# Projecting 32 sample tokens of two mixers in plain fp32 by four column groups

## The chip, the cores and the metric

The kernel runs on one core of a Trainium2 chip. The metric is the device time of one execution in microseconds (us), lower is better. Engines are named PE (TensorE), DVE (VectorE), ACT (ScalarE), POOL (GpSimd) and SP (SyncE, which here only issues DMAs).

## The reference

One inference step of a two-layer encoder for two request groups: 512 prompt tokens and 32 sample tokens with a cache of 256 past rows. What matters here is the start of each mixer:

```python
h = _rmsnorm(x, norm_mix[l]) * (1.0 + sc1) + sh1
# even layer: 4 differential-attention heads, 8 stick-breaking heads
proj = h @ w_in_even        # (T, 1024) @ (1024, 3072)
# odd layer: 16 forgetting-attention heads, and 16 gate logits
q, k, v, fl = jnp.split(h @ w_in_odd, [FOX_W, 2 * FOX_W, 3 * FOX_W], axis=-1)
logf = jax.nn.log_sigmoid(fl + b_f)
```

The same weights project both groups. Attention, output projection, a mixture of 16 experts and a final norm follow; their code does not change, apart from one count on which the output weights' load waits. Everything is fp32 in and out.

## The kernel before

**Product.** The 544 tokens are five row tiles: four of 128 prompt tokens (t = 0 to 3) and one with the 32 sample tokens (t = 4, `NT`), padded to 128 columns. The 3072 weight columns are cut into `NB` = 8 blocks of `BW` = 384 (128 each of q, k, v). A product of one tile with one block is numbered n = 5b + t. It is made to fp32 accuracy from three products of rounded parts (`split_product`, L563 to L565): high by high, high by low, low by high, over 8 slices k of the contraction, so 24 matmuls with 128 stationary and 384 moving columns, into `bank[n % 2]`. The sample tile takes the same 24 as a prompt tile. ACT rounds each raw weight quarter (`fuse_high`, L612), DVE makes the rest (`fuse_low`, L618); the raw block lies in one buffer, `fu_raw`, that SP fills with 8 DMAs (`fuse_load`, L603) once the lows of the block before are made. ACT copies the tiles t = 0, 2, 4 of a block out of the banks (L661), DVE the tiles 1 and 3 (L668).

**Order.** Everything is ordered by hand. Each mixer has a lead and then 40 units u = 5i + t (block i, tile t). In the lead (`lead_pe`) the normed rows are turned by PE transposes, in the order sample tile, then prompt tiles 0 to 3, each turned tile rounded into `hT` (ACT, `row_high`, L494) and `hT2` (DVE, `row_low`, L500); products 0 to 4 are put between. In the odd layer the gate logits (`gate_logits`) stand before product 4. Then in unit u PE does the attention of unit u while product u + 6 is cut into three pieces (slices 0-2, 2-6, 6-8; 0-4, 4-6, 6-8 where t = 0) which stand between attention steps: next scores, piece, turn or later sums, piece, values, piece. So the product of the sample tile of block i + 2 stands in the unit t = 3 of block i. Attention uses L849, L863, L886 (differential), L895 to L949 (stick-breaking) and L1447 to L1485 (forgetting); ACT's copies L1041, L1076 and L1550 feed the values.

**Beside it.** The conditioning rows of coming layers are computed in the same units by `ada_matvec` (L326) and `ada_sum` (L332): 8 plain fp32 matmuls of 32 stationary and 512 moving columns in four column groups, whose weights (2 MB a chunk) also come through SP's queue. Each plain fp32 matmul stands as two records in the trace. In the even mixer POOL's queue carries cache loads and stores of new rows; in the odd one SP's.

Of the kernel before, what the change touches and what calls it, by code (L numbers as in the profile page):

```python
# [21 lines left out]
P = 128  # L22
# [53 lines left out]
def encoder_step(nc, a, out, rope_dram):  # L76
    ctx = ExitStack()
    with ctx:
# [51 lines left out]
        upto = sb("upto", [P, P])  # L130
# [8 lines left out]
        c_in = sb("c_in", [P, 2, KD])  # L139
        ss = sb("ss", [P, 8])  # L140
# [58 lines left out]
        def setup_pool(pool):  # L199
# [7 lines left out]
            pool.memset(upto[:, :], 1.0)  # L207
# [11 lines left out]
            for m in (ident, ident_b):  # L219
# [5 lines left out]
                               pattern=[[1, P]], channel_multiplier=-1)  # L225
            pool.affine_select(out=upto[:, :], in_=upto[:, :], compare_op=ALU.is_ge, fill=0.0, base=0,
# [204 lines left out]
        NORM = sems("norm", "square", "rstd", "scaled", "shifted", "tr", "ev_a", "ev_v", "self", "gain", "shift_v", "pad")  # L431
# [70 lines left out]

        def row_pool(pool, l):
            s, o = NORM, 2 * l
            for flat in (hT_flat, hT2_flat):
                pool.tensor_copy(r32(flat[:, KD * TOK:HT_LEN]), ones[:, 0:P - DEC]).then_inc(s["pad"], 1)
# [26 lines left out]
        def lead_pe(pe, l, last_logits=None):  # L533

            row_turn(pe, l, 0)
            row_turn(pe, l, 1)
            row_turn(pe, l, 2)
            for t in range(TILES):
                row_evicted(pe, l, min(t + 1, TILES - 1))
                if t == NT:  # L540
                    pe.wait_ge(NORM["pad"], 2 * l + 2)
                    if last_logits:
                        last_logits()
                fuse_product(pe, l, t, 0, KD)
                if t + 3 < TILES:
                    row_turn(pe, l, t + 3)

# [29 lines left out]
        FU = sems("fu", "raw0", "raw1", "hi", "lo", "mm", "ev_a", "ev_v")  # L577
# [4 lines left out]
        fu_lo = [ring_flat[:, 2 * KD * BW * i + KD * BW:2 * KD * BW * (i + 1)] for i in range(2)]  # L582
        by_row = lambda v: v.rearrange("p (k c) -> p k c", k=KD)
# [21 lines left out]
        def fuse_high(act, l, b, q):  # L605
# [3 lines left out]
            if b >= 2:  # L609
                act.wait_ge(FU["mm"], TILES * (g_b - 1))  # L610
# [9 lines left out]
        def fuse_product(pe, l, n, k0, k1):  # L620

            if n >= NB * TILES:
                return
            b, t = n // TILES, n % TILES
            hi, lo = r32(by_row(fu_hi[b % 2])), r32(by_row(fu_lo[b % 2]))
            for k in range(k0, k1):
                if t == 0 and k % 2 == 0:
                    pe.wait_ge(FU["lo"], 4 * (NB * l + b) + k // 2 + 1)
                if k == 0 and n >= 2:
                    fuse_rows_out(pe, l, n - 2)  # L630
# [4 lines left out]

        def fuse_rows_out(eng, l, n):

            g_b, t = NB * l + n // TILES, n % TILES
            if t % 2 == 0:
                eng.wait_ge(FU["ev_a"], 3 * g_b + t // 2 + 1)  # L640
            else:
                eng.wait_ge(FU["ev_v"], 2 * g_b + t // 2 + 1)

# [12 lines left out]
        def fuse_rows_act(act, l, n):  # L656
            b, t = n // TILES, n % TILES
            if n < NB * TILES and t % 2 == 0:
                act.wait_ge(FU["mm"], UNITS * l + n + 1)
                fuse_rows_free(act, l, b)  # L660
                act.activation(fu_rows[b % 2][0:rows(t), t, :], bank[n % 2][0:rows(t), 0:BW], ACT.Copy).then_inc(FU["ev_a"], 1)  # L661

        def fuse_rows_dve(dve, l, n):
            b, t = n // TILES, n % TILES
            if n < NB * TILES and t % 2 == 1:
                dve.wait_ge(FU["mm"], UNITS * l + n + 1)
                fuse_rows_free(dve, l, b)
                dve.tensor_copy(fu_rows[b % 2][0:rows(t), t, :], bank[n % 2][0:rows(t), 0:BW]).then_inc(FU["ev_v"], 1)  # L668
# [75 lines left out]
        def even_pool(pool):  # L744
# [13 lines left out]
            def store(b):  # L758
                pool.wait_ge(FU["ev_a"], 3 * b + 3)
                pool.wait_ge(FU["ev_v"], 2 * b + 2)  # L760
# [37 lines left out]
        def even_pe(pe):  # L798
# [7 lines left out]
            def turn_q_k(i):  # L806
# [4 lines left out]
                else:  # L811
                    pe.wait_ge(FU["ev_a"], 3 * i + 2)
                    pe.wait_ge(FU["ev_v"], 2 * i + 2)
# [4 lines left out]
            def turn_rest(i):  # L818
                if i < N_DIFF:
                    pe.wait_ge(F0["roped"], 2 * i + 2)  # L820
                else:
                    pe.wait_ge(FU["ev_a"], 3 * i + 3)
# [199 lines left out]
        def even_act(act):  # L1022
# [109 lines left out]
            row_high(act, 0, 2)  # L1132
            fuse_rows_act(act, 0, 0)
# [5 lines left out]
            fuse_rows_act(act, 0, 4)  # L1139
            q_out(0)  # L1140
            late_out(0)
            for u in range(UNITS):
                i, t = u // TILES, u % TILES
# [1480 lines left out]
```

## Time and profile before

| | |
|---|---|
| median of 3 runs | 1740.81 us (1735.86 to 1748.72) |
| profiled execution, its own time | 1750.45 us |
| its span in the trace | 1748.7 us |
| PE busy | 1486.2 us (85%) |
| DVE busy | 1032.4 us (59%) |
| ACT busy | 865.5 us (49%) |
| POOL busy | 489.7 us (28%) |
| TensorE granted clock, mean | 0.924 |

Times inside the execution are counted from the span's start. The even mixer runs from about 50 to 418 us, the odd one from about 898 to 1279 us. "Busy" PE records overlap, because matmuls are pipelined: a matmul's length in the trace holds its latency, and what it costs is the distance from its start to the start of the next.

### The profile page before, as it was taken

The numbers are of one execution on the slowest core, as the hardware profiler recorded it, in microseconds if no ns is written. First come the engines' busy times: TensorE is split into PE (matmuls) and PEld (weight loads), VectorE is DVE, ScalarE is ACT, GpSimd is POOL, SyncE is SP. The second block draws the span as 40 slices with busy tenths as digits, with TensorE's granted clock in tenths as the row PEclk, the third lists the DMA queues.
The fourth block names the chain that finished last, engine by engine and source line by source line (L and its number), as shares of the span: only waits on it lengthen the run. The fifth ranks groups of instructions, "written<-read, shape, count | busy, mean of one in ns | idle before, by whom it ended". The sixth has DMA issues, their size and how long they took to land.

```text
span 1748.7 us, 22798 instructions
## 1 busy us (share of the span) xinstructions
PE 1486.2 (85%) x7979; PEld 1162.0 (66%) x7979; DVE 1032.4 (59%) x1345; ACT 865.5 (49%) x1512; POOL 489.7 (28%) x379
## 2 busy tenths in 40 slices
PE   3499999997947999999937899999889399999981
PEld 0387777764735777877727677777567277878770
DVE  0555442224446988988956443333363568888995
ACT  2233334445124777777733333333341267788772
POOL 1200111110104666656521000000001155656650
PEclk8699999998967999999968999999989599999995
DMA  8435553133044899989970333443420479999984
GB/s 279 147 120 180 187 170 104 68 124 106 1 195 154 337 351 356 369 342 354 357 249 12 98 104 104 129 136 114 155 75 36 167 263 344 367 367 364 335 314 170
DMA packets 148608, 358.62 MB, mean 205 GB/s; under 512 B 18660, under 2 KB 80868, under 8 KB 122420
## 3 DMA queue, kind: packets, MB, share of 16 engines
q1 hardware_dynamic: 136184, 333.25, 52.7%
q0 software_dynamic: 12352, 24.40, 3.8%
q8 instruction: 45, 0.74, 0.2%
q14 instruction: 27, 0.22, 0.0%
HBM read 341.87 MB, written 33.56 MB: 215 GB/s over the span
## 4 chain that ended last, share of the span: by engine, by line
PE 65%; DVE 12%; issue 7%; ACT 6%; DMA 5%; SPq 2%; DVEq 1%; POOL 0%; POOLq 0%; ACTq 0%; PEldq 0%; PEld 0%
PE bank L563 17%; PE bank L565 15%; PE bank L564 15%; DVE ring_r L1945 4%; DMA ring<-in_w_gate 2%; PE bank L326 2%; ACT work_r L1938 2%; PE bank L1447 2%; PE bank L1485 1%; PE bank L676 1%; PE bank L332 1%; PE bank L1462 1%; PE bank L2231 1%; PE bank L919 1%; PE bank L558 1%
## 5 line engine op out<-in xcount | busy, mean ns | idle before, releaser
L564 PE MATMUL bank<-ring_r,arena_r 128*128 128x512 f32 x816 | 323.6, 397 | 0.0
L563 PE MATMUL bank<-ring_r,hT_r 128*128 128x384 f32 x640 | 239.9, 375 | 1.6 <-ACT hT_r L494 1.6
L564 PE MATMUL bank<-ring_r,hT_r 128*128 128x384 f32 x640 | 217.0, 339 | 0.0
L565 PE MATMUL bank<-ring_r,work_r 128*128 128x384 f32 x640 | 217.0, 339 | 0.0
L1945 DVE TENSOR_TENSOR ring_r<-ring,work_r 128x1024 fp32r<-128x1024 f32 x102 | 177.2, 1763 | 28.2 <-ACT work_r L1938 28.2
L1945 DVE TENSOR_TENSOR ring_r<-ring,arena_r 128x1024 fp32r<-128x1024 f32 x96 | 166.4, 1771 | 29.3 <-ACT arena_r L1938 29.3
L564 PEld LDWEIGHTS bank<-ring_r,arena_r 128*128 128x128 f32 x816 | 157.3, 193 | 31.1
L1945 DVE TENSOR_TENSOR ring_r<-ring,hT_r 128x1024 fp32r<-128x1024 f32 x108 | 155.1, 1464 | 25.1 <-ACT hT_r L1938 24.3
L1938 ACT ACTIVATE hT_r<-ring 128x1024 fp32r<-128x1024 f32 x144 | 144.3, 1054 | 47.3 <-DMA ring<-in_w_gate 41.5
L563 PEld LDWEIGHTS bank<-ring_r,hT_r 128*128 128x128 f32 x640 | 121.7, 190 | 43.0 <-issue 39.1
L1938 ACT ACTIVATE work_r<-ring 128x1024 fp32r<-128x1024 f32 x136 | 136.6, 1059 | 6.9 <-DMA ring<-in_w_up 6.8
L1938 ACT ACTIVATE arena_r<-ring 128x1024 fp32r<-128x1024 f32 x128 | 126.8, 1052 | 21.6 <-DMA ring<-in_w_down 21.3
L1889 POOL TENSOR_TENSOR arena<-arena,bc 128x1024 f32<-128x1024 f32 (+1 forms) x6 | 14.3, 2382 | 434.9 <-DVE arena L1875 434.9
L563 PE MATMUL bank<-hT_r,arena_r 128*128 128x512 f32 x288 | 123.2, 428 | 8.9 <-DVE arena_r L2386 5.6
L564 PEld LDWEIGHTS bank<-ring_r,hT_r 128*128 128x128 f32 x640 | 122.2, 191 | 1.2 <-issue 0.7
L565 PEld LDWEIGHTS bank<-ring_r,work_r 128*128 128x128 f32 x640 | 121.3, 190 | 0.0
L565 PE MATMUL bank<-hT_r,arena_r 128*128 128x512 f32 x288 | 118.4, 411 | 0.0
L2421 POOL TENSOR_TENSOR ring_r<-ring,arena_r 128x1024 fp32r<-128x1024 f32 x32 | 86.3, 2696 | 90.9 <-ACT arena_r L1938 90.9
L563 PE MATMUL bank<-work_r,arena_r 128*128 128x512 f32 x272 | 109.2, 402 | 0.0
L2421 POOL TENSOR_TENSOR ring_r<-ring,hT_r 128x1024 fp32r<-128x1024 f32 x36 | 92.4, 2566 | 54.0 <-ACT hT_r L1938 40.4
L563 PE MATMUL bank<-arena_r 128*128 128x512 f32 x256 | 100.9, 394 | 6.7 <-DVE ring_r L1945 6.6
L565 PE MATMUL bank<-work_r,arena_r 128*128 128x512 f32 x272 | 106.4, 391 | 0.0
(356 smaller groups left out, 2880.3 us busy)
## 6 DMA issues: line engine op xcount, KB each, us to landing
ring<-in_w_gate SPq DMA_DIRECT2D x68, 1024.0 KB, 6.8
ring<-in_w_up SPq DMA_DIRECT2D x68, 1024.0 KB, 7.4
ring<-in_w_down SPq DMA_DIRECT2D x68, 1024.0 KB, 7.5
bc<-in_w_ada SPq DMA_DIRECT2D x40, 1024.0 KB, 6.8
bc<-in_w_in_even SPq DMA_DIRECT2D x64, 192.0 KB, 4.0
bc<-in_w_in_odd SPq DMA_DIRECT2D x64, 192.0 KB, 3.6
ring<-in_w_ada SPq DMA_DIRECT2D x4, 2048.0 KB, 12.3
arena<-moe_out SPq DMA_DIRECT2D x8, 1024.0 KB
```

Source lines behind the costliest of these rows:

```text
L326: last = nc.tensor.matmul(acc[32 * q:32 * q + 32, :], silu_c[:, 4 * h + q, :], ada_w[h][:, q, :], start=h == 0, stop=h == 1)
L332: nc.tensor.matmul(acc[0:32, :], pick[:, :], ada_part(pre), start=True, stop=True).then_inc(AD["sum"], 1)
L558: last = nc.tensor.matmul(acc, wr[:, k, :], hT[:, k, cols(t)], start=k == 0, stop=k == KD - 1)
L563: nc.tensor.matmul(acc, rows_hi, w_hi, start=first, stop=False)
L564: nc.tensor.matmul(acc, rows_hi, w_lo, start=False, stop=False)
L565: return nc.tensor.matmul(acc, rows_lo, w_hi, start=False, stop=last)
L676: last = nc.tensor.transpose(out_bank[0:np_, c:c + r], src, ident[0:r, 0:r])
L919: last = nc.tensor.matmul(b[:, 0:n], neg_from[:, :], s[:, 0:n], start=False, stop=True, skip_group_check=True)
L1447: nc.tensor.matmul(fx_bank(u, h)[0:r, 0:n], fx_qT[i % 2][half, cols(t)], fx_kT[i % 2][half, k0:k0 + n], start=True, stop=False)
L1938: act.activation(r32(piece(m_high[v], q)), piece(m_low[v], q), ACT.Copy).then_inc(MO[f"hi_{c}"], 1)
L1945: dve.tensor_tensor(r32(piece(m_low[v], q)), piece(m_low[v], q), f32(piece(m_high[v], q)), ALU.subtract).then_inc(MO[f"lo_{c}"], 1)
L2421: pool.tensor_tensor(r32(piece(m_low[v], 1)), piece(m_low[v], 1), f32(piece(m_high[v], 1)), ALU.subtract).then_inc(MO[f"lop_{c}"], 1)
```

## The change

The sample tile is no longer projected with the 24 split matmuls. DVE copies the turned sample rows unrounded into `sample_T` (two copies in each lead). A new `fuse_sample` multiplies them with the raw fp32 block: for each slice k four matmuls, each with the 32 sample tokens stationary and a quarter (96) of the block's columns moving, written to partitions 32q to 32q + 31 of one bank. The raw block therefore has to be there until that product is done: `fuse_load` waits for it too. The sample product moves one block ahead: that of block 0 is made in the lead after the third turn, in bank 6, and that of block b + 1 stands where the sample tile of block b stood (n = 5b + 4, cut into the same three pieces); the last such place, in the unit t = 3 of block 6, is empty. ACT evicts it with four copies of 32 by 96, `sample_rows`, at the start of the unit t = 0 one block later. The gate logits move before product 3. In the odd lead DVE evicts tile 3 after the last two weight quarters, and copies the first k rows (`k_out(0)`) after the gate chain. Counts of semaphores follow. Unused `upto` is dropped.

```diff
 def row_sample(dve, l):
+    for half in range(2):
+        dve.wait_ge(s["ev_a"], EV_A[o] + half + 1)
+        dve.tensor_copy(sample_T[:, 4 * half:4 * half + 4, :], row_turned(0, half)).then_inc(s["smp"], 1)
@@ lead_pe
             row_turn(pe, l, 1)
+            pe.wait_ge(NORM["smp"], 2 * l + 2)
             row_turn(pe, l, 2)
-            for t in range(TILES):
-                row_evicted(pe, l, min(t + 1, TILES - 1))
-                if t == NT:
-                    pe.wait_ge(NORM["pad"], 2 * l + 2)
-                    if last_logits:
-                        last_logits()
+            fuse_sample(pe, l, 0, bank[6], 0, KD)
+            for t in range(NT):
+                row_evicted(pe, l, t + 1)
+                if t == NT - 1 and last_logits:
+                    last_logits()
                 fuse_product(pe, l, t, 0, KD)
                 if t + 3 < TILES:
                     row_turn(pe, l, t + 3)
+            fuse_product(pe, l, NT, 0, KD)
@@ fuse_load
                 sp.wait_ge(FU["lo"], 4 * g_b)
+                sp.wait_ge(FU["smp"], g_b)
@@ fuse_product
+            if b + t // NT >= NB:
                 return
+            if k0 == 0 and n >= 2:
+                fuse_rows_out(pe, l, n - 2)
+            if t == NT:
+                fuse_sample(pe, l, b + 1, bank[n % 2], k0, k1)
+                return
+        def fuse_sample(pe, l, b, acc, k0, k1):
+            w = by_row(fu_raw)
+            for k in range(k0, k1):
+                if k % 4 == 0:
+                    pe.wait_ge(FU[f"raw{k // 4}"], 64 * (NB * l + b) + 64)
+                for q in range(4):
+                    last = nc.tensor.matmul(acc[DEC * q:DEC * (q + 1), 0:SW], sample_T[:, k, :], w[:, k, SW * q:SW * (q + 1)],
+                                            start=k == 0, stop=k == KD - 1)
+            if k1 == KD:
+                last.then_inc(FU["smp"], 1)
+        def sample_rows(act, l, b, acc):
+            act.wait_ge(FU["smp"], NB * l + b + 1)
+            fuse_rows_free(act, l, b)
+            for q in range(4):
+                act.activation(fu_rows[b % 2][0:DEC, NT, SW * q:SW * (q + 1)], acc[DEC * q:DEC * (q + 1), 0:SW],
+                               ACT.Copy).then_inc(FU["ev_s"], 1)
@@ even_act and fox_act, the units
+                if t == 0 and 1 <= i < NB - 1:
+                    sample_rows(act, l, i + 1, sample_bank(i + 1))
                 fuse_rows_act(act, l, u + TILES)
@@ fox_dve
             fuse_low(dve, 1, 1, 1)
-            fuse_rows_dve(dve, 1, 3)
...
             fuse_low(dve, 1, 1, 3)
-            k_out(0)
+            fuse_rows_dve(dve, 1, 3)
...
             dve.drain().then_inc(FG["dve"], 1)
+            k_out(0)
             maxima(0)
```

## Rows read from the trace of the kernel before

**Rows 1.** Windows over the units of both mixers: window, length, busy time by engine, clock, DMA.

```profile
103.00:263.00 160.00, 160.00 (x984) 122.39 (x985) 77.96 (x204) 59.55 (x169) 18.25 (x28) 1.00 0.50 170
...
975.00:1263.00 288.00, 280.52 (x1910) 212.15 (x1910) 106.80 (x256) 104.40 (x315) 0.00 (x0) 0.98 0.38 121
```

**Rows 2.** Timeline of PE, odd mixer, unit t = 3 of block 2: start, length, instruction.

```profile
1084.15 0.45 PE L563 MATMUL bank<-ring_r,hT_r 128*128 128x384 f32 x1
...
1085.32 1.04 PE L1462 MATMUL bank<-ident,arena 128*128 128x128 f32 x8
...
1087.26 0.45 PE L563 MATMUL bank<-ring_r,hT_r 128*128 128x384 f32 x1
...
1089.56 1.09 PE L1485 MATMUL bank<-arena 128*64 128x128 f32 x16
1090.58 0.44 PE L563 MATMUL bank<-ring_r,hT_r 128*128 128x384 f32 x1
...
1092.80 0.27 PE L676 MATMUL bank<-ident,arena 128*128 128x128 f32 x1
```

**Rows 3.** Timeline of ACT, odd mixer, same unit.

```profile
1086.01 1.09 ACT L1550 ACTIVATE arena<-bank 128x512 f32<-128x512 f32 x2 [0.18 <-PE bank L1462]
```

**Rows 4.** Timeline of PE, differential part of the even mixer, unit t = 3 of block 1.

```profile
169.46 0.42 PE L563 MATMUL bank<-ring_r,hT_r 128*128 128x384 f32 x1
...
171.64 1.05 PE L886 MATMUL bank<-arena 128*128 128x128 f32 x8
172.45 0.42 PE L563 MATMUL bank<-ring_r,hT_r 128*128 128x384 f32 x1
...
173.68 0.62 PE L332 MATMUL bank<-bc,pick 128*32 128x512 f32 x1
```

**Rows 5.** Timeline of ACT, same unit.

```profile
169.74 0.60 ACT L1041 ACTIVATE arena<-bank 128x512 f32<-128x512 f32 x1
```

**Rows 6.** Timelines of PE and ACT, stick-breaking part, unit t = 3 of block 5.

```profile
333.22 0.63 PE L563 MATMUL bank<-ring_r,hT_r 128*128 128x384 f32 x1
...
335.70 1.08 PE L942 MATMUL bank<-arena 128*64 128x512 f32 x4
...
333.71 0.60 ACT L1076 ACTIVATE arena<-bank 128x512 f32<-128x512 f32 x1 [0.85 <-PE bank L929]
```

**Rows 7.** Timeline of PE: one conditioning product in four column groups, and what follows.

```profile
125.92 1.92 PE L326 MATMUL bank<-bc,silu_c 128*32 128x512 f32 x16
127.78 0.44 PE L563 MATMUL bank<-ring_r,hT_r 128*128 128x384 f32 x1
```

**Rows 8.** Timeline of PE: the short values of a sample unit in two column groups.

```profile
1097.13 0.66 PE L1485 MATMUL bank<-arena 128*64 128x32 f32 x12
1097.71 0.49 PE L1447 MATMUL bank<-arena 64*128 64x128 f32 x4
```

**Rows 9.** Sources: all weight loads of L326, count, durations in ns (min/median/max).

```profile
L326 PEld LDWEIGHTS bank<-bc,silu_c x320: 106/110/178, 110.2 to 1262.3; 128*32 128x32 f32 x160
```

**Rows 10.** Timeline of PE, lead of the even mixer: third turn and first product.

```profile
71.66 1.97 PE L526 MATMUL bank<-ident,arena 128*128 128x128 f32 x8 [1.65 <-POOL arena L511]
75.24 0.66 PE L563 MATMUL bank<-ring_r,hT_r 128*128 128x384 f32 x1 [1.62 <-ACT hT_r L494]
```

**Rows 11.** Timelines of PE, lead of the odd mixer: product 0, next turn, first scores.

```profile
932.62 0.67 PE L563 MATMUL bank<-ring_r,hT_r 128*128 128x384 f32 x1
...
937.95 1.03 PE L526 MATMUL bank<-ident,arena 128*128 128x128 f32 x8
...
975.29 0.38 PE L1447 MATMUL bank<-arena 64*128 64x128 f32 x2 [4.21 <-ACT logf L1599]
```

**Rows 12.** Window over product 0 of that lead.

```profile
932.60:938.00 5.40, 5.40 (x27) 5.37 (x26) 5.33 (x6) 2.40 (x6) 0.00 (x0) 0.78 0.00 0
```

**Rows 13.** Timelines of SP's queue and ACT: a raw block's 8 loads, and their first use.

```profile
173.28 4.16 SPq L603 DMA_DIRECT2D bc<-in_w_in_even  x8
...
183.61 0.85 ACT L612 ACTIVATE ring_r<-bc 128x768 fp32r<-128x768 f32 x1
```

More of the change, by code:

```diff
@@ L429, in encoder_step @@
         junk = arena[:, 14336:15360]
-        NORM = sems("norm", "square", "rstd", "scaled", "shifted", "tr", "ev_a", "ev_v", "self", "gain", "shift_v", "pad")
+        NORM = sems("norm", "square", "rstd", "scaled", "shifted", "tr", "ev_a", "ev_v", "self", "gain", "shift_v", "smp")
         NORM_NO = {"norm_mix0": 0, "norm_ffn0": 1, "norm_mix1": 2, "norm_ffn1": 3}
@@ L505, in row_pool @@
             for flat in (hT_flat, hT2_flat):
-                pool.tensor_copy(r32(flat[:, KD * TOK:HT_LEN]), ones[:, 0:P - DEC]).then_inc(s["pad"], 1)
+                pool.tensor_copy(r32(flat[:, KD * TOK:HT_LEN]), ones[:, 0:P - DEC])
             for j in (0, 2, 4):
@@ L657, in fuse_rows_act, with sample_bank @@
             b, t = n // TILES, n % TILES
-            if n < NB * TILES and t % 2 == 0:
-                act.wait_ge(FU["mm"], UNITS * l + n + 1)
+            if n < NB * TILES and t in (0, 2):
+                act.wait_ge(FU["mm"], NT * (NB * l + b) + t + 1)
                 fuse_rows_free(act, l, b)
-                act.activation(fu_rows[b % 2][0:rows(t), t, :], bank[n % 2][0:rows(t), 0:BW], ACT.Copy).then_inc(FU["ev_a"], 1)
+                act.activation(fu_rows[b % 2][:, t, :], bank[n % 2][:, 0:BW], ACT.Copy).then_inc(FU["ev_a"], 1)
         def fuse_rows_dve(dve, l, n):
             b, t = n // TILES, n % TILES
-            if n < NB * TILES and t % 2 == 1:
-                dve.wait_ge(FU["mm"], UNITS * l + n + 1)
+            if n < NB * TILES and t in (1, 3):
+                dve.wait_ge(FU["mm"], NT * (NB * l + b) + t + 1)
                 fuse_rows_free(dve, l, b)
-                dve.tensor_copy(fu_rows[b % 2][0:rows(t), t, :], bank[n % 2][0:rows(t), 0:BW]).then_inc(FU["ev_v"], 1)
+                dve.tensor_copy(fu_rows[b % 2][:, t, :], bank[n % 2][:, 0:BW]).then_inc(FU["ev_v"], 1)
+        def sample_bank(b):
+            return bank[6] if b == 0 else bank[(TILES * b - 1) % 2]
         def fx_bank(u, h):
@@ L1601, in fox_act @@
                 i, t = u // TILES, u % TILES
+                if t == 0 and 1 <= i < NB - 1:
+                    sample_rows(act, 1, i + 1, sample_bank(i + 1))
                 fuse_rows_act(act, 1, u + TILES)
@@ L1664, in fox_dve @@
             row_shift(dve, 1, 1)
+            row_sample(dve, 1)
             row_low(dve, 1, 0)
```

62 lines of the change are left out of this document (34 added, 28 removed).

## The prediction

> **What bounds the kernel now.** I read the windows over the mixers first. In the differential units PE is busy for the whole window, in the units of the odd mixer for 280.5 of 288 us, both at the full clock, while DVE, ACT and the DMA engines are busy for half of it or less [rows 1]. What remains is to see whether the piece that the change shortens is really paid for by PE, so I went on to the timeline of PE in a unit t = 3, the unit whose filler is the sample product. In the odd mixer (block 2) its first piece runs from 1084.15 to the turn at 1085.32, 1.17 us; its middle piece from 1087.26 to the values at 1089.56, 2.30 us; its last one follows the values and merges with the first piece of the next product, 1090.58 to 1092.80, 2.22 us for both [rows 2]. In the even mixer the last piece stands alone: the middle one costs 2.18 us, the last 1.23 us [rows 4]. No idle time is marked before any of these. Then ACT, to see how early what PE needs next is there: the values of the odd unit need two copies that end at 1087.10, and PE comes for them 2.46 us later [rows 3, 2]. The differential ones need a copy that ends at 170.34, PE comes at 171.64 [rows 5, 4]; the stick-breaking ones one that ends at 334.31, PE comes at 335.70 [rows 6]. So PE bounds these units, with 1.3 to 2.5 us of slack behind the middle piece.
>
> **What the new product costs.** The nearest rows are the conditioning products: the same form, 32 stationary columns, four column groups, plain fp32, 8 matmuls as 16 records, but 512 moving columns. The whole takes 127.78 - 125.92 = 1.86 us [rows 7]. Were the records run one after another, each would have 0.12 us for 512 columns, less than the product's records of 384 columns take at the full clock (12 in 2.18 us, 0.18 each [rows 4]); so I read it that four run side by side, and there are four rounds. I split the 1.86 us into 0.15 for going into and out of the groups and four rounds of 0.427. With 96 columns a round is 0.427 x 96 / 512 = 0.080 us. The sample product has 64 records, 16 rounds, 1.28 us; cut into three pieces (4, 8 and 4 rounds) it pays 0.15 three times: pieces of 0.47, 0.79, 0.47, **1.73 us** in all. That is the lower bound, short of an overlap still better than in rows 7. The upper one is from the shortest grouped records of the trace, values with 32 columns in two groups: 12 records, six rounds, in 0.58 us; less the 0.15, 0.072 a round, where streaming would ask for 0.027 [rows 8]. If that is four instructions (two loads, two matmuls) being issued, a round of eight takes 0.144 us, and the product 2.75 us. I take 1.73, since rows 7 have the same groups, the same eight instructions a round, and the nearer length.
>
> The Trainium skill, TensorEngine Tiling (Array Packing), Instruction Overhead, puts some 60 cycles on every matmul; taken as an estimate, 64 records one behind the other at 25 ns would be 1.6 us plus the three entries, 2.05 us, and the forecast would be 4 us later. Rows 7 show no such charge beside the streaming, though their long matmuls could hide it.
>
> **Steady state, odd mixer.** Per sample product: before, 1.17 + 2.30 + 2.22 = 5.69 us with the next product's first piece; after, 1.73 + 1.2 for that piece alone (as the first piece here). 2.76 us saved. Does the slack hold? The turn ends and `ada_sum` (0.98 us from its start to the next piece [rows 2]) stands between it and the piece, so the values come 1.5 us earlier with respect to ACT's copies, out of 2.46: yes. Six such places: 16.6 us. The seventh place is empty now: all 5.69 go but 1.2, 4.5 us, with PE then just behind ACT. Together **21.1 us**.
>
> **Even mixer.** Differential, four places: first piece 1.15 by likeness, 0.68 saved; last 1.23 - 0.47 = 0.76. The middle piece could fall by 1.39, but slack is 1.30 less about 0.1 for the signal, so 1.2. 2.64 us each, 10.6. Stick-breaking, two places: slack 1.39, the same 1.3 for the middle, 2.7 each, 5.4. The empty place: 1.15 + 1.23 + 1.3 = 3.7. Together **19.7 us**.
>
> **Leads.** In the even one product 4 (24 records at 0.18, 4.2 us) gives way to the sample product of block 1 in one piece, 1.28 + 0.15 = 1.4: 2.8 saved. That of block 0 is new. PE sits idle 1.62 us between the third turn (from 71.66, about 2 us) and product 0 at 75.24 [rows 10], and it comes there, at the lower clock, 1.2 GHz (the eight transposes before it take 1.97 us, later ones 1.03 [rows 10, 11]): 2.56 + 0.3 = 2.9 us, 1.3 more than the gap. Product 0 itself now runs partly at that clock (5.33 us in the odd lead at a mean 0.78 [rows 11, 12] against 4.2), so 1.2 us of it comes back if the clock rises during the new product instead. Net 2.5 saved.
> In the odd lead there is no gap: the sample product of block 0 delays product 0 by 2.9, DVE's two copies before the third turn by 0.4, the clock gives back 1.2: 2.1 us later. The gate logits move ahead of product 3, 4.2 earlier, and product 4 is gone. The first scores at 975.29 waited 4.21 us for ACT's last copy of the gate chain [rows 11], so that chain decides, and it starts 2.1 earlier. In it `k_out(0)`, which stood ahead of the forget chain on DVE and waits for PE's transposes, moves behind it; the eviction of tile 3 stands there instead and comes earlier. I price this at 0 to 4 us and take 1.9: 4.0 in sum, at which PE's own work (product 3, sample, product 5, transposes) ends at the same time as the chain. Both leads **6.5 us**.
>
> **Costed at nothing.** The four evictions on ACT (about 0.6 us) stand before a copy for which ACT waits on PE anyway; the bank that they free is needed a piece later. DVE's copies in the even lead fall where it waits for POOL. SP: the raw block's load waits now for the sample product, too. Its eight issues, 173.28 to 177.44, begin when the sample product's last piece (172.45 to 173.68) is ending [rows 4, 13]; that piece will end about 2.6 us sooner, so the old gate stays the later one. First use is at 183.61 [rows 13], 6.2 us after the last issue; minus 2.6 there are 3.6 left for it. Behind the load stand on SP the conditioning weights, in the odd mixer past rows too. In both leads the load of block 1 moves behind the first sample product, with over 5 us in hand. The stores wait for sample rows that come a block earlier. Without `upto` POOL's setup is shorter, off the path.
>
> **Sum.** 21.1 + 19.7 + 6.5 = 47.3, I take 47. The profiled execution 1750.45 becomes 1703; it stands 9.6 above the median of the runs shown, and from the median, 1740.81, I get **1694 us**. Bounds: at 2.75 us a product 14 places lose 1 us and the first two about 1 each, 16 us less; leads at their worst 4 less: 1714. Better: no stall behind the middle pieces and the full chain gain, 5 more: 1689. The runs shown spread over 13 us, 6 either way: 1683 to 1718 as range, the far end short of the two bounds together with the spread.
>
> **Rivals.**
> *The groups run one after another* (slower). If matmuls in one bank on the same columns exclude each other, and each pays rows 8's 0.045 over its streaming: 64 x 0.125 + 0.45 = 8.45 us against 4.7. Twelve places +3.8, one lead product +4, the first ones +6 each, less the 8.2 of the empty places: +53, 1794 us. It turns slower from about 5.2 us a product; serial at bare streaming, 5.6, is 1750. Against: rows 7 write the same bank's same columns. 4%.
> *Loads of weights don't hide* (1719). A load of 32 columns lasts 0.110 us [rows 9]; if each round waits for it, a round is 0.190 and the product 3.5 us, 25 less gained. Against: rows 7 leave no room for four such waits within 0.15 us. 4%. The Trainium skill, TensorE: Matmul & The Clock Gate, The mechanism, says that weight loads overlap running matmuls only if the row group differs (it also allows the background buffer); all groups here share the rows, so by the strict reading this rival would hold, and the trace speaks against it.
> *The units are bound by their chain* (1717). ACT, DVE and PE pass a unit's data around; if shorter pieces meet it everywhere, only first and last pieces gain, 1.4 x 12, plus 6.5 from leads. For: slack is small in the even mixer; against: rows 2 and 3. 6%.
> *The raw load comes late* (1721). If the sample product's end gates the load and the rest of SP's queue comes behind, ACT blocks in `fuse_high` ahead of the probabilities, 2 us a block over 14 blocks. Against: the 3.6 us. 5%.
> The forecast's mechanism: 81%.
>
> **Chances.** A measurement of this kernel tells about 1%, 17 us, from no change. Faster by more: forecast and three rivals, less some of their lower ends, 92%. Within 1%: 4%. Slower: 4%.
>
> **What would show it.** Right: 64 records a product, starting in fours; 1.3 to 1.4 us in the leads; units t = 3 shorter by 2.7; the odd mixer's first scores 4 us sooner after its third turn. Wrong: L1485, L886 or L942 with idle time before them in unit t = 3; L612 waiting for DMA beyond block 0's one; rounds of over 0.1 us. The forecast fails if a round takes more than 0.144 us, or if a lead's chain eats what the units give.

## The result and the profile after

The changed kernel takes 1697.26 us (median of 4 runs, 1694.26 to 1700.78) against 1741.49 us for the kernel before on the same chip (4 runs, 1735.86 to 1748.72). The ratio is 0.9741, with a 95% interval of 0.9715 to 0.9767: 44 us less, where 47 were forecast.

The first lines of the profile's page show less PE work in more instructions (before: 1486.2 us in 7979).

```profile
span 1699.0 us, 24152 instructions
PE 1439.4 (85%) x8611; PEld 1115.0 (66%) x8619; DVE 1022.3 (60%) x1349; ACT 872.2 (51%) x1560; POOL 491.1 (29%) x377
```

The profiled spans differ by 49.7 us. To see how much of that is the change, I cut PE's timeline at eight starts, four in each mixer: the first turn, the first and the last `ada_matvec` (it recurs in the same units of every block, so it marks the block's period), and the first matmul of the output projection.

| us | before | after | difference | forecast |
|---|---|---|---|---|
| even mixer, lead (first turn to first `ada_matvec`) | 43.16 | 40.95 | -2.2 | -2.5 |
| even mixer, units (to the last `ada_matvec`) | 295.88 | 277.63 | -18.3 | -19.7 |
| odd mixer, lead | 75.81 | 73.45 | -2.4 | -4.0 |
| odd mixer, units | 266.17 | 244.22 | -22.0 | -21.1 |
| ends of both (to the output projection) | 40.25 | 41.24 | +1.0 | 0 |
| **mixers together** | 721.3 | 677.5 | **-43.8** | -47.3 |
| all other work up to PE's last matmul | 988.1 | 982.0 | -6.1 | 0 |

The last row cannot be put down to the change. Nothing there was edited in any kernel of this study, apart from the one count on which the output weights' load waits, and it came out between 972.6 and 988.7 us over all of them. A few microseconds of the change's effect could hide in that. So below, mechanisms are judged by the sum over the mixers, and the medians only where they differ by more.

The mixers scatter too, and one place where they do is the last period of the odd units, the one with the empty place. Windows over it in the kernel before and in the changed one (columns as in [rows 1]; the clock is the third number from the end):

```profile
1228.15:1260.60 32.45, 28.75 (x205) 19.66 (x204) 11.10 (x30) 11.30 (x38) 0.00 (x0) 0.93 0.34 119
...
1188.40:1216.07 27.67, 22.74 (x180) 14.70 (x179) 11.09 (x30) 10.71 (x37) 0.00 (x0) 1.00 0.56 196
```

The changed kernel ran it wholly at the full clock, and the kernel before did not. Four of the experiments below leave this stretch as it is and still did not run it wholly at the full clock: there it took 28.5 to 29.0 us at a mean of 0.91 to 0.94, and 29.50 at 0.87. So some 1 us of the 22.0 in the odd units is the clock of this execution and not the smaller product. (The last period of the even units is alike: a mean of 0.95 before, 1.00 after.)

**The unit that the change shortens.** Timeline of PE, changed kernel, odd mixer, unit t = 3 of block 2 (columns as in [rows 2], whose unit this is):

```profile
1055.85 0.54 PE L652 MATMUL bank<-bc,sample_T 128*32 128x96 f32 x16
1056.32 1.09 PE L1505 MATMUL bank<-ident,arena 128*128 128x128 f32 x8
1057.34 0.62 PE L329 MATMUL bank<-bc,pick 128*32 128x512 f32 x1
1057.36 0.37 PE L652 MATMUL bank<-bc,sample_T 128*32 128x96 f32 x6
1057.80 0.59 PE L329 MATMUL bank<-bc,pick 128*32 128x512 f32 x1
1058.22 0.82 PE L652 MATMUL bank<-bc,sample_T 128*32 128x96 f32 x26
1058.98 1.09 PE L1528 MATMUL bank<-arena 128*64 128x128 f32 x16
1060.00 0.54 PE L652 MATMUL bank<-bc,sample_T 128*32 128x96 f32 x16
1060.47 0.44 PE L567 MATMUL bank<-ring_r,hT_r 128*128 128x384 f32 x1
```

From start to start, the first piece costs 0.47 us (1055.85 to 1056.32) where it was 1.17, and the last one 0.47. No idle time is marked before the values, L1528. The period of a block falls from 38.95 to 36.09 us, six times by 2.86. In the stick-breaking part it falls from 44.42 to 41.73, in the differential one from 38.33 to 36.25 us.

In the differential unit the values now do wait, for ACT's copy of the turn. Timeline of PE from the next unit's scores (L889) on, and then ACT's exponentials of those scores (L1071) and its copy, block 1 as in [rows 4, 5]:

```profile
162.03 0.68 PE L889 MATMUL bank<-arena 64*32 64x288 f32 x4
162.64 0.54 PE L652 MATMUL bank<-bc,sample_T 128*32 128x96 f32 x16
163.11 0.66 PE L903 MATMUL bank<-ident,arena 128*128 128x128 f32 x4
163.69 0.87 PE L652 MATMUL bank<-bc,sample_T 128*32 128x96 f32 x32
164.87 1.16 PE L926 MATMUL bank<-arena 128*128 128x128 f32 x8 [0.31 <-ACT arena L1081]
165.96 0.54 PE L652 MATMUL bank<-bc,sample_T 128*32 128x96 f32 x16
166.31 1.02 PE L329 MATMUL bank<-bc,pick 128*32 128x512 f32 x2
...
163.28 0.49 ACT L1071 ACTIVATE arena<-bank,small 32x288 f32<-32x288 f32 x1 [6.31 <-DVE small L1225]
...
164.15 0.18 ACT L1071 ACTIVATION_READ_ACCUMULATOR arena<-bank,small 32x1 f32 x1
164.25 0.57 ACT L1081 ACTIVATE arena<-bank 128x512 f32<-128x512 f32 x1
```

The copy ends at 164.82, the values start at 164.87. The copy stands on ACT right behind the exponentials, and these waited for DVE's maxima of the scores (L1225). So what the values wait for begins with the scores and not with the turn: they start 2.84 us after the scores (162.03 to 164.87), where the kernel before, whose copy had 1.3 us to spare, came to them after 4.29. Its scores (the values start at 171.64 [rows 4]):

```profile
167.35 0.68 PE L849 MATMUL bank<-arena 64*32 64x288 f32 x4
```

**The whole product in one piece**, in the two leads: at the lower clock in the first place, at the full one in the second. Timelines of PE, even and odd mixer, each with the matmul that follows:

```profile
72.54 2.79 PE L652 MATMUL bank<-bc,sample_T 128*32 128x96 f32 x64
75.26 0.69 PE L567 MATMUL bank<-ring_r,hT_r 128*128 128x384 f32 x1
...
943.08 1.53 PE L652 MATMUL bank<-bc,sample_T 128*32 128x96 f32 x64
944.54 0.44 PE L567 MATMUL bank<-ring_r,hT_r 128*128 128x384 f32 x1
```

That is 2.72 and 1.46 us, against 4.2 for the 24 split matmuls. The sources view of the line has the length of its weight loads (ns, minimum/median/maximum):

```profile
L652 PEld LDWEIGHTS bank<-bc,sample_T x1024: 106/110/178, 72.5 to 1168.5; 128*32 128x32 f32 x171
```

64 loads of 110 ns are 7.0 us, in a product that lasts 1.46. So the loads run beside each other and beside the matmuls, though all four groups use the same rows.

**The start of the odd units.** Timeline of PE, lead and first units, without the product's rows:

```profile
951.40 0.49 PE L1490 MATMUL bank<-arena 64*128 64x128 f32 x4 [0.49 <-issue]
...
962.34 0.69 PE L1528 MATMUL bank<-arena 128*64 128x128 f32 x4 [5.62 <-ACT arena L1593]
```

The scores no longer wait for the gate chain (4.21 us in [rows 11]). But the values of unit 0 wait 5.62 us. The next fence, ACT and SP's queue of the same stretch, says for what:

```profile
960.20 0.84 ACT L618 ACTIVATE ring_r<-bc 128x768 fp32r<-128x768 f32 x1 [6.87 <-DMA bc<-in_w_in_odd]
961.85 0.44 ACT L1593 ACTIVATE arena<-bank 128x128 f32<-128x128 f32 x2
...
951.33 0.38 SPq L1418 DMA_DIRECT2D out_fox_logf_p<-logf  x1
953.86 0.50 SPq L1409 DMA_DIRECT2D out_fox_v_s<-arena  x1
954.46 4.09 SPq L609 DMA_DIRECT2D bc<-in_w_in_odd  x8
```

ACT rounds the first quarter of raw block 2 ahead of the turned probabilities, and block 2's load stands on SP behind the stores of the gate rows and of the first state; the gate rows are what the gate chain ends with. The kernel before has the same stall, 3.49 us long:

```profile
985.63 0.44 PE L1485 MATMUL bank<-arena 128*64 128x128 f32 x4 [3.49 <-ACT arena L1550]
...
983.49 0.84 ACT L612 ACTIVATE ring_r<-bc 128x768 fp32r<-128x768 f32 x1 [6.24 <-DMA bc<-in_w_in_odd]
```

### The profile page after: what moved, and what is told of

It reads as the page before. It is cut to its first block, busy times and chain, and to the rows that moved or that the text cites. A ratio compares the mean times of both kernels' runs of the same rounds, so it can differ in the third digit from the quotient of the medians.

```text
span 1699.0 us, 24152 instructions
## 1 busy us (share of the span) xinstructions
PE 1439.4 (85%) x8611; PEld 1115.0 (66%) x8619; DVE 1022.3 (60%) x1349; ACT 872.2 (51%) x1560; POOL 491.1 (29%) x377
## 4 chain that ended last, share of the span: by engine, by line
PE 64%; DVE 11%; issue 8%; DMA 7%; ACT 6%; SPq 2%; DVEq 1%; POOLq 0%; ACTq 0%; PEldq 0%; POOL 0%; PEld 0%
PE bank L567 15%; PE bank L569 14%; PE bank L568 14%; DVE ring_r L1992 3%; DMA ring<-in_w_gate 3%; PE bank L323 2%; PE bank L1490 2%; PE bank L1528 2%; ACT work_r L1985 2%; PE bank L652 1%; PE bank L717 1%; DMA ring<-in_w_up 1%; PE bank L1505 1%; PE bank L329 1%; PE bank L2278 1%
## 5 line engine op out<-in xcount | busy, mean ns | idle before, releaser
L567 PE MATMUL bank<-ring_r,hT_r 128*128 128x384 f32 x512 | 191.9, 375 | 0.0
L569 PE MATMUL bank<-ring_r,work_r 128*128 128x384 f32 x512 | 173.1, 338 | 0.0
L568 PE MATMUL bank<-ring_r,hT_r 128*128 128x384 f32 x512 | 172.9, 338 | 0.0
L1992 DVE TENSOR_TENSOR ring_r<-ring,hT_r 128x1024 fp32r<-128x1024 f32 x108 | 150.1, 1418 | 26.8 <-ACT hT_r L1985 25.9
L567 PEld LDWEIGHTS bank<-ring_r,hT_r 128*128 128x128 f32 x512 | 96.9, 189 | 30.9 <-issue 28.5
L567 PE MATMUL bank<-arena_r 128*128 128x512 f32 x256 | 100.9, 394 | 6.1 <-DVE ring_r L1992 5.8
L569 PE MATMUL bank<-arena_r 128*128 128x512 f32 x256 | 99.8, 390 | 0.0
L568 PEld LDWEIGHTS bank<-ring_r,hT_r 128*128 128x128 f32 x512 | 97.4, 190 | 0.8 <-issue 0.7
```

The costliest lines, as they stand in the source:

```text
L567: nc.tensor.matmul(acc, rows_hi, w_hi, start=first, stop=False)
L568: nc.tensor.matmul(acc, rows_hi, w_lo, start=False, stop=False)
L569: return nc.tensor.matmul(acc, rows_lo, w_hi, start=False, stop=last)
L1992: dve.tensor_tensor(r32(piece(m_low[v], q)), piece(m_low[v], q), f32(piece(m_high[v], q)), ALU.subtract).then_inc(MO[f"lo_{c}"], 1)
```

## The experiments

The runs behind the first comparison came in three groups, each on one chip beside the kernel before. One column group, gate logits back, load early and first sample product earlier ran beside 1745.43 us; whole product in the middle piece, before with load early, load early with gate logits back and all three beside 1744.02; the three marked "again" beside 1743.50. The last two columns are of the one profiled execution.

| kernel | median us | ratio to before | mixers | all other |
|---|---|---|---|---|
| before (profile) | | | 721.3 | 988.1 |
| changed | 1697.26 | 0.9741 [0.9715, 0.9767] | 677.5 | 982.0 |
| changed again | 1696.53 | 0.9723 [0.9696, 0.9750] | 676.9 | 980.3 |
| one column group | 1757.02 | 1.0060 [1.0029, 1.0091] | 739.8 | 981.8 |
| gate logits back | 1696.37 | 0.9704 [0.9647, 0.9762] | 677.2 | 972.6 |
| load early | 1684.82 | 0.9632 [0.9594, 0.9671] | 670.2 | 979.4 |
| load early again | 1691.40 | 0.9696 [0.9668, 0.9724] | 668.9 | 978.5 |
| load early, gate logits back | 1694.50 | 0.9716 [0.9676, 0.9757] | 674.5 | 988.4 |
| first sample product earlier | 1691.16 | 0.9677 [0.9636, 0.9717] | 672.8 | 976.1 |
| whole product in the middle piece | 1691.62 | 0.9697 [0.9662, 0.9733] | 672.6 | 979.6 |
| before, with load early | 1744.15 | 0.9988 [0.9949, 1.0028] | 717.1 | 985.2 |
| load early, first earlier, middle | 1685.01 | 0.9656 [0.9622, 0.9690] | 661.9 | 988.7 |
| the same three again | 1683.17 | 0.9655 [0.9630, 0.9681] | 666.8 | 977.2 |

**One column group.** The same 32 matmuls with the same operands, all four quarters written to partitions 0 to 31 (at other columns of the bank), where ACT's copies then read them.

```diff
-                    last = nc.tensor.matmul(acc[DEC * q:DEC * (q + 1), 0:SW], ...,
-                                            start=k == 0, stop=k == KD - 1)
+                    last = nc.tensor.matmul(acc[0:DEC, SW * q:SW * (q + 1)], ...,
+                                            start=k == 0 and q == 0, stop=k == KD - 1 and q == 3, ...)
```

> All four quarters of a sample product are written to the same partitions 0 to 31, at different columns of the bank, so that all 64 records use one column group and can only run one after another; all else as in the changed kernel. Theory (four groups run side by side, PE is what the units pay for): a record streams 0.080 us, a product takes at least 5.1 us instead of 1.46 in one piece, 14 products in the units and leads on PE's path cost 3.7 more each, the two first ones up to 5: about +55 to +65 us on the changed kernel, 1750 to 1765, so slightly slower than before. Rival (the groups contribute little, the gain comes from the smaller padding alone): 1697 to 1710. Rival (the units are bound by their chain, not by PE): under +25.

Measured: 1757.02 us, and periods of 40.01 (odd), 39.80 (differential) and 45.66 us (stick-breaking), all longer than before the change (38.95, 38.33, 44.42). Timeline of PE, odd unit t = 3, of block 1, middle piece and values:

```profile
1058.08 2.80 PE L652 MATMUL bank<-bc,sample_T 128*32 128x96 f32 x32
1060.82 1.09 PE L1528 MATMUL bank<-arena 128*64 128x128 f32 x16
```

32 records take 2.73 us, 0.085 each, and 64 in the lead 5.40 us against 1.46: the four groups do run side by side, 3.7 times faster than one. Here too 64 loads of 110 ns, 7.0 us, fit into 5.40. It is the rival "groups one after another", realised: it needed about 5.2 us a product to turn slower, this one takes 5.4 to 5.6 and is slower. Without the groups the smaller product gains nothing.

**Gate logits back.** Behind product 3 again, with DVE's eviction of tile 3 ahead of the gate chain.

```diff
-                if t == NT - 1 and last_logits:
-                    last_logits()
                 fuse_product(pe, l, t, 0, KD)
...
+            if last_logits:
+                last_logits()
             fuse_product(pe, l, NT, 0, KD)
```

> The changed kernel with the gate logits back behind product 3 (ahead of the sample product of block 1), DVE's eviction of tile 3 back ahead of its wait for them. Theory (the gate chain decides when the odd mixer's units start, PE's own lead work ends just with it): the gate chain starts 4.2 us later, product 3 no longer covers it, the first scores come 3 to 4 us later: about 1700.5, PE idle 3 to 4 us before the first scores. Rival (what bounds the start of the odd mixer is the load of block 2's raw weights, which stands on SP behind the gate rows): the same 3 to 4 us, since that load waits for the same rows. Rival (the move was worth nothing): within 1 us of the changed kernel.

Measured: no difference (mixers 677.2 against 677.5). The first scores do come 2.7 us later after the first turn (55.70 us instead of 53.01), but the first `ada_matvec` does not (73.35 against 73.45). Timeline of PE, and windows from the first scores to the turn of unit 0 and from the values to the first `ada_matvec`:

```profile
944.39 0.80 PE L1490 MATMUL bank<-arena 64*128 64x128 f32 x4 [3.25 <-ACT logf L1643]
...
954.79 0.44 PE L1528 MATMUL bank<-arena 128*64 128x128 f32 x4 [2.23 <-ACT arena L1593]
```

```profile
944.39:951.13 6.74, 6.74 (x28) 5.52 (x29) 1.89 (x7) 1.08 (x5) 0.00 (x0) 0.52 0.69 184
954.79:962.04 7.25, 7.25 (x49) 5.70 (x49) 3.83 (x9) 2.47 (x7) 0.00 (x0) 1.00 0.76 273
```

The same two windows of the changed kernel:

```profile
951.40:955.29 3.89, 3.89 (x29) 3.27 (x30) 1.80 (x7) 1.08 (x5) 0.00 (x0) 1.00 0.57 152
962.34:971.84 9.50, 9.50 (x48) 6.87 (x48) 3.82 (x9) 2.46 (x7) 0.00 (x0) 0.73 0.49 184
```

The wait for the chain is back (3.25 us), and the wait behind it is 3.39 us shorter. But that alone is not why nothing changes. The load stands behind the gate rows, which come later too, and so the values come 2.15 us later after the first turn (66.10 for 63.95), much as the rival on the load had it. What gives this back is the clock. Here it was low behind the first wait (6.74 us for 3.89), a stretch behind which PE waits for the load anyway, and full behind the values. In the changed kernel it was low behind the long wait of the values, which costs 2.25 us (9.50 for 7.25). The expectation missed, since it did not price the clock.

**Load early.** Raw block 2 issued ahead of SP's wait for the gate rows (the place in the loop goes).

```diff
+            fuse_load(sp, 1, 2)
             sp.wait_ge(FG["act"], FG_ACT["rows"])
...
-                if i + 2 < NB:
+                if 1 <= i < NB - 2:
                     fuse_load(sp, 1, i + 2)
```

> The changed kernel with the raw load of block 2 of the odd mixer issued before SP waits for the gate rows, not after the stores of block 0. Theory A (that load is what keeps the units from starting: PE stands for 6.9 us minus one piece in unit 0 because ACT waits for it ahead of its probabilities): the stall goes, 6 to 8 us less, about 1690; the next thing late may be the conditioning weights of that block. Theory B (the lead gave less than forecast because of the new first sample product at the lower clock): this changes nothing, within 1.5 us of the changed kernel.

Measured: the stall is gone, and the first `ada_matvec` comes 65.06 us after the first turn, 8.4 sooner. That is more than the stall of 5.62 us: behind it, values to `ada_matvec` take 7.23 us at a mean clock of 1.00, where the changed kernel took 9.50 at 0.73. The load is issued 6.6 us ahead of the gate rows; SP's queue, then PE's values of unit 0, with no idle time marked:

```profile
938.51 4.09 SPq L609 DMA_DIRECT2D bc<-in_w_in_odd  x8
945.12 0.38 SPq L1419 DMA_DIRECT2D out_fox_logf_p<-logf  x1
...
950.44 0.33 PE L1529 MATMUL bank<-arena 128*64 128x128 f32 x2
```

The mixers gain 7.3 us, since the last period of the odd units gives 1.8 back, at the lower clock shown above. The median fell by 12.4; the repeat below gave 5.1, so the rest of the 12.4 is not the load's.

**Load early in the kernel before.** The same edit there.

> The kernel before, with one edit: in the odd mixer the raw load of block 2 is issued ahead of the wait for the gate rows, not behind the gate rows' and the first state's store. Theory: the wait of the first unit of block 0 for that load was there before the change (TensorE waited 3.5 us in it), so the edit alone brings the kernel before from 1741 to about 1736, and takes the first ada_matvec of the odd mixer 4 to 6 us nearer to its first turn (75.81 us before). Rival: the stall is one of the changed kernel alone, made by its earlier start of the scores: 1741 and 75.8.

Measured: the lead falls from 75.81 to 70.45 us and the mixers by 4.1 us. The median doesn't show it (0.9949 to 1.0028 holds both 0 and 4 us). So the stall is older than the change, as the theory has it; that the whole kernel gets faster by it stays unconfirmed.

**Load early, gate logits back.** Both edits, to see what the move of the gate logits is worth once the load doesn't hide it.

> The changed kernel with the raw load of block 2 early (1684.82 in the run before) and, in addition, the gate logits back behind product 3 and DVE's eviction of tile 3 back ahead of the gate chain. Theory: the move of the gate logits is worth what the first scores come later without it (2.7 us), and the load alone had hidden that: with the load early it shows, so 1687 to 1688, first turn to first ada_matvec 67.5 to 68 instead of 65.06. Rival: the move is worth nothing in either, since another wait (TensorE waits for the evicted block 0 or its copies) stands in that place: 1685, 65.

Measured: 71.06 us from first turn to first `ada_matvec` instead of 65.06, 6.0 later, twice the theory's 2.7. Timeline of PE, and then the window from the first scores to the turn of unit 0 (columns as in [rows 1]), in this kernel:

```profile
957.77 0.80 PE L1491 MATMUL bank<-arena 64*128 64x128 f32 x4 [3.25 <-ACT logf L1644]
```

```profile
957.77:964.52 6.75, 6.75 (x28) 5.53 (x29) 3.45 (x11) 2.84 (x10) 0.00 (x0) 0.52 0.68 193
```

The same window of the kernel with the load early alone:

```profile
945.19:949.07 3.88, 3.88 (x28) 3.27 (x29) 2.36 (x8) 2.67 (x10) 0.00 (x0) 1.00 0.61 163
```

The same 28 records take 6.75 us instead of 3.88, at a mean granted clock of 0.52, nearly all at the lower level, instead of 1.00. The wait of 3.25 us for the gate chain costs itself (the scores come 3.1 later) and 2.9 more behind it.

**First sample product earlier.** In both leads it stands ahead of the third turn, where PE waits anyway.

```diff
             pe.wait_ge(NORM["smp"], 2 * l + 2)
-            row_turn(pe, l, 2)
             fuse_sample(pe, l, 0, bank[6], 0, KD)
+            row_turn(pe, l, 2)
```

> The changed kernel with the sample product of block 0 put ahead of the third turn, where PE has nothing to do, in both leads. Theory B (the first sample product delays product 0 at the lower clock): in the odd lead all 2.7 us of it come back, in the even one some 1 to 2: 3 to 5 us less, about 1693. Theory A (the odd lead's end is set by the gate chain and the load behind it): the gate chain starts earlier by the same 2.7, so the same 3 to 5 us. Rival (the clock falls back between the turns and product 0 so that it pays what the move saves): within 1.5 us.

Measured: mixers 4.7 us less, the odd lead 3.1 and the even one 1.6 of it; product 0 of the odd mixer comes 14.39 us after the first turn instead of 17.41, nearly back at the 14.00 of before. There the sample product no longer delays anything; what PE waits for is POOL:

```profile
901.28 1.97 PE L529 MATMUL bank<-ident,arena 128*128 128x128 f32 x8 [3.38 <-POOL arena L514]
```

**Whole product in the middle piece.** In the units t = 3 of both mixers all eight slices stand in the middle place, none in the first and last (the odd mixer's lines are shown).

```diff
-                    k = 4 if t == 0 else 2
+                    whole = n % TILES == NT
+                    k = 0 if whole else 4 if t == 0 else 2
                     fuse_product(pe, 1, n, 0, k)
...
-                    fuse_product(pe, 1, n, k, 6)
+                    fuse_product(pe, 1, n, k, KD if whole else 6)
```

> In the unit t = 3 of every block in both mixers, the whole sample product stands in the unit's middle piece (all eight k, where the changed kernel has k 0-1, 2-5 and 6-7 in three places). Theory: each place where the sample records stand among other TensorE work costs its neighbours 0.1 to 0.3 us (in the changed kernel the stall inside the middle piece of 1.175 us, the turns before it 0.587 and the values behind it 1.088 us, against 0.80, 0.36 and 0.81 without it). One place instead of three then gives 0.7 to 0.9 us per differential unit, 0.3 per stick-breaking and per odd unit: the periods of the differential blocks go from 36.25 to about 35.5 us, and the total from 1697 to about 1692. Rival: the places cost nothing and the missing 0.56 us per differential block are waits of the chain, which stay: 1697, periods as in the changed kernel. Rival: the unit's chain had the pieces as its cover, and waits open where they stood: 1700.

Measured: 5.0 us less in the mixers, but a good part of it is not the edit's. The periods fall by 0.33 (differential, where 0.75 was expected), 0.27 (odd) and 0.24 us (stick-breaking), some 3 us over all places. Yet the units as a whole are only 1.6 us shorter, as the last odd period took 28.79 us at a mean clock of 0.94. The other 3.4 us lie in the leads and ends, which the edit does not touch, and are taken for scatter. Timeline of PE and then ACT's copy, differential unit of block 1:

```profile
161.48 0.68 PE L889 MATMUL bank<-arena 64*32 64x288 f32 x4
162.09 0.66 PE L903 MATMUL bank<-ident,arena 128*128 128x128 f32 x4
162.67 1.53 PE L652 MATMUL bank<-bc,sample_T 128*32 128x96 f32 x64
164.32 1.16 PE L926 MATMUL bank<-arena 128*128 128x128 f32 x8
...
163.69 0.57 ACT L1083 ACTIVATE arena<-bank 128x512 f32<-128x512 f32 x1
```

No idle time is marked before the values, but they still start 0.06 us after the copy ends (164.26), and 2.84 us after the scores, as in the changed kernel. So scores, DVE, ACT and copy still decide when the values start. What the edit gives here is the last piece, 0.35 us in the changed kernel (165.96 to 166.31), which now stands in time that PE had to wait through. In the odd units, which did not wait, 0.27 us is about what two entries less are worth at the prediction's 0.15 each.

The turn still takes 0.58 us (162.09 to 162.67) and the values 1.09. In the kernel before, the values took 0.81 us, and the turn 0.35, from this row to the piece at 169.46 [rows 4]:

```profile
169.11 0.60 PE L863 MATMUL bank<-ident,arena 128*128 128x128 f32 x4
```

So full-width matmuls next to the sample records take 0.2 to 0.3 us more than next to the split ones, wherever the product is cut.

**All three.** Early load, first sample product earlier, whole product in the middle.

> The changed kernel with the raw load of block 2 early, the leads' sample product ahead of the third turn of rows, and the sample product of the unit t = 3 whole in the middle piece. If the three add up: 12.4 less for the load, 3 to 6 less for the leads, 5 less for the middle piece, so about 1675 to 1681. Rival: the lead's product 0 ahead only moves TensorE into a wait for the gate chain, and the last odd interval gives back 1 to 2 us: 1682 to 1685.

The median, 1685.01 us, was no better than that of the early load alone on another chip, while the mixers were at 661.9, 15.6 below the changed kernel (the three edits' own gains, 7.3, 4.7 and 5.0, add up to 17.0). Only runs on one chip could settle that, hence the last three.

> The changed kernel itself, once more. In the runs so far the two mixers (from the first turn of a lead to the start of the output projection) took 721.3 us before and 677.5 us after the change, and agreed to 0.3 us between profiles where nothing in them was edited, while everything outside the mixers took 972.6 to 988.7 us in profiles whose edits don't touch it. Theory: that is a property of single executions, so here the mixers take 677 to 678 again, the rest anything from 972 to 989, and the median is 1692 to 1700. Rival: the rest goes by the kernel's build, so it comes out at 982 again.

> The changed kernel with the raw load of block 2 early, once more, beside the changed kernel. If its gain is what the mixers showed (677.5 to 670.2), the median is 7 us below the changed kernel's of this call; if the first comparison (12.4 us) was the load's alone, it is 12 below.

> All three edits together (early load, sample product before the third turn in the leads, the sample product whole in the middle piece), once more. By the mixers (677.5 to 661.9) the median is 15 us below the changed kernel's of this call and 8 below that with the early load alone. Rival, from the medians so far (1685.01 against 1684.82 in another call): no better than the early load alone, because what it gives in the mixers is taken back outside them.

Measured, on one chip: 1696.53, 1691.40 and 1683.17 us. By the medians the early load is worth 5 us (by the mixers 7.3 and 8.0), all three 13 us. The rival that the gain is given back outside the mixers falls: the same kernel spent 988.7 us there in one profile and 977.2 in the other. The mixers agree less well than the 0.3 us in the expectation of the first of them: 661.9 and 666.8 us for the same kernel. In the second, PE waited in the even mixer for DVE's sum of a conditioning row, for which the bias row's DMA came late, and the last period of each mixer's units ran partly at the lower clock (mean 0.95 and 0.88 instead of 1.00), which makes 3.2 us of the 4.9. The late wait is this row of PE's timeline:

```profile
240.87 0.30 PE L717 MATMUL bank<-ident,arena 128*128 128x128 f32 x1 [0.91 <-DVE ada_row L339]
```

## Why the prediction was right, and where its terms were off

**PE bounds the units outside the differential ones, and the groups run side by side: shown, and with it two rivals are refuted, groups one after another and loads that don't hide.** Undoing only the groups turned 44 us less into 12 us more. The read of [rows 7], 0.15 us for entering and leaving and 0.080 a round, gave 1.43 us for the product in one piece; it measured 1.46. The bound from [rows 8], 0.144 a round, was far off. The estimate from the page's charge came nearer: The Trainium skill, TensorEngine Tiling (Array Packing), Instruction Overhead, gives some 60 cycles to a matmul, and charged to each record, one behind the other, as the prediction did, that is 1.6 us by itself; here the whole product takes 1.46. The Trainium skill, TensorE: Matmul & The Clock Gate, The mechanism, lets a load overlap a running matmul where the row group differs, or where it goes to the background buffer. The strict reading, by row group alone, does not hold here: with the same rows throughout, 7.0 us of loads fit into the same 1.46, and in one column group into 5.40. Which buffer they went to, no run shows.

**Odd units: 21.1 forecast, 22.0 measured.** 2.86 a block for 2.76, and 4.8 for 4.5 at the empty place. The 0.1 more is `ada_sum`: it and the middle piece took 1.64 us together (1057.34 to 1058.98), where 0.98 and 0.79 had been added up. The 4.8 is partly luck. It compares 32.45 us at a mean clock of 0.93 with 27.67 at 1.00; against the changed code at 0.91 to 0.94 it is 3.5 to 4.0.

**Even units: 19.7 forecast, 18.3 measured.** Stick-breaking was right (2.69 against 2.7), and the empty place gave more (4.8 against 3.7; 4.4 at the like clock of 0.95, 36.38 to 32.00 us, the latter in "changed again"). The term that was off is the differential one, 2.64 forecast, 2.08 measured. From the scores to the values it was to gain 0.68 at the first piece and 1.2 at the middle one, 1.88; it gained 1.45 (4.29 to 2.84). I had counted the copy's slack of 1.3 us as belonging to the middle piece alone, as if a shorter first piece brought the turn and with it the copy forward. But the copy stands behind ACT's exponentials, which hang on the scores, ahead of both pieces. It came only 0.2 us sooner after them (2.79 for 2.99), so both pieces had to share the slack. That much of the rival "bound by their chain" is true, and it is the idle time before L886 that the prediction listed as a sign of being wrong. The kernel with the whole product in the middle bears it out, with the same 2.84. The turn's 0.23 us beside the sample records cost nothing here, since it falls into that wait. The 0.28 of the values does cost, as I had charged the entry to the column groups only to the pieces themselves; the last piece, 0.35 for 0.47, gives 0.12 back.

**Leads: 6.5 forecast, 4.6 measured.** Even: 2.2 for 2.5 (the terms given, 2.8 less 1.3 and 1.2 back, add up to 2.7). Odd: the first scores came 3.7 us sooner after the first turn, near the 4.0 forecast, and behind no wait but issue. But only 2.4 of it reached the units: the stretch from the scores to the values took 0.6 longer, since the stall in it grew by 2.1 us and the full clock ahead of it gave only 1.5 back, and the one from the values to `ada_matvec` took 0.7 longer, at a mean clock of 0.73 for 0.81. "The raw load comes late" stood among the rivals for the units, gated by the sample product; there it did not happen (ACT waits for a DMA in L618 once in the whole execution). It happened behind the scores of unit 0: the load of block 2 is gated by the gate rows on SP, in both kernels. The prediction knew of this wait ("beyond block 0's one") and set it aside. I listed SP's queue as costed at nothing with "in the odd mixer past rows too", and did not ask what those rows wait for, nor what the wait would do to scores that come sooner. The row of the kernel before, 3.49 us of idle time at 985.63, was there to be read.

**The gate logits' move** is worth nothing as the kernel stands and 4 to 6 us once the load is early (mixers 670.2 and 668.9 against 674.5, leads 65.06 against 71.06). I had priced it at 4.2 less what follows; the runs show 3.1 for the wait and 2.9 for the clock behind it.

**The total** was right because the largest term, the units, was priced from the right mechanism and the right rows. That it came within 3.5 us in the mixers is in part luck: about 4 us too much in the differential places and the odd lead stands against some 1.5 too little at the two empty places, and about as much as that came there from the clock. And the time outside the mixers scatters by more than all of this.

## What to carry to other kernels

When few rows meet many columns, cut the columns over the column groups: it multiplied the rate by 3.7 where cutting without groups would have lost, and price one round from any grouped product that the trace already holds. When a step on the path gets earlier, follow every queue that its successor reads from, and not only that of the moved step: where two waits follow each other, removing the first lengthened the second by as much here, and the low clock only changed its place. Count slack from the instruction that the waited-for work really hangs on, or it is spent twice. And compare small gains by landmarks within the stage, in several profiles, since here the untouched stages alone moved by 16 us.

## What the runs showed of the hardware that was not expected

- A matmul in one column group doesn't keep the records of other groups waiting: the two records of `ada_sum`, 512 columns each in one group, started at 1057.34 and 1057.80, and six sample records started between them, from 0.02 us behind the first.
- Side by side, a round of four records takes 0.091 us (1.46 over 16, the entry included); with one column group a single record takes 0.084 (5.40 over 64). So four cost hardly more than one.
- After 3.25 us of waiting, the next 6.75 us ran at a mean granted clock of 0.52, and cost 2.9 us; the wait nearly doubled. It is not the same each time: after the 4.21 us in the kernel before [rows 11], the next 5.61 us ran at a mean of 0.70.
- In the differential units, full-width turns and values next to such records take 0.23 and 0.28 us longer. Why was not tested.
